# Decay and rate products, their sigmoids and cumulative sums inside the units of v, and two swapped buffers in the RWKV-7 scan

## What is computed

```python
rkv = einsum('btsd,sde->btse', xs[:, :, :3], w_rkv)          # r, k, v: three products of 1024 x 1024
logw = -softplus(-(w0 + tanh(xw @ w1) @ w2)) - 0.5           # decay
a = sigmoid(a0 + (xa @ a1) @ a2)                             # rate
kk = l2_normalize(heads(k * k_k))
k = k * (1.0 + (a - 1.0) * k_a)
y, s = rwkv7_recurrence(r, exp(-exp(logw)), k, v, -kk, kk * a, s0)   # heads of 64
# in the recurrence, for each token:
S = S * w_t + (S a_t) b_t + v_t k_t ;  y_t = S r_t
```

## Time and profile before

| | us |
|---|---|
| runs of the kernel before (3) | 2781.00, 2783.11, 2784.36 |
| median | 2783.11 |
| the profiled execution | 2780.13 |
| its span, first to last instruction | 2777.8 |
| PE busy in it | 2630.7 (95%) |

### The profile page before, as it was taken

The page is one execution under the profiler, slowest core; times in us unless marked ns, Lnnn a source line. Parts: engine busy times, 40 slices in busy tenths (PEclk is TensorE's granted clock), DMA queues, the critical chain, the costliest instruction groups (busy, mean ns, idle before and its releaser), DMA issues. The chain is left out here.

```text
span 2777.8 us, 62146 instructions
## 1 busy us (share of the span) xinstructions
PE 2630.7 (95%) x27185; PEld 2548.2 (92%) x27185; DVE 1146.0 (41%) x1458; ACT 892.2 (32%) x1281; POOL 1014.4 (37%) x478
## 2 busy tenths in 40 slices
PE   9999999997899999999999999999588889999998
PEld 8999998997888999999999999899378859999998
DVE  3333127845554533321533322631754455433313
ACT  4222224233323422222422222333533333422222
POOL 2444432332434244444244443133034352344442
PEclk9999999999998999999999999899689999999999
DMA  4222222221013222222222222122000022222321
GB/s 151 83 91 92 94 72 73 91 67 39 2 51 112 75 90 84 91 100 75 73 86 86 96 94 80 43 92 89 1 3 4 4 78 80 63 89 86 105 84 54
DMA packets 55195, 202.98 MB, mean 73 GB/s; under 512 B 6384, under 2 KB 8560, under 8 KB 55024
## 3 DMA queue, kind: packets, MB, share of 16 engines
q1 hardware_dynamic: 55024, 200.38, 22.0%
HBM read 190.68 MB, written 9.67 MB: 72 GB/s over the span
## 5 line engine op out<-in xcount | busy, mean ns | idle before, releaser
L317 POOL TENSOR_TENSOR wlo<-raw,whi 128x1024 fp32r<-128x1024 f32 (+1 forms) x261 | 709.0, 2716 | 1018.7 <-ACT whi L282 1018.7
L346 PE MATMUL ps<-xh,whi 128*128 128x272 f32 x3568 | 1031.2, 289 | 6.1 <-POOL wlo L317 4.2
L348 PE MATMUL ps<-xh,wlo 128*128 128x272 f32 x3568 | 1034.7, 290 | 0.0
L347 PE MATMUL ps<-xl,whi 128*128 128x272 f32 x3568 | 1027.3, 288 | 0.0
L346 PEld LDWEIGHTS ps<-xh,whi 128*128 128x128 f32 x3568 | 673.1, 189 | 9.5 <-issue 6.8
L347 PEld LDWEIGHTS ps<-xl,whi 128*128 128x128 f32 x3568 | 674.1, 189 | 0.0
L348 PEld LDWEIGHTS ps<-xh,wlo 128*128 128x128 f32 x3568 | 672.0, 188 | 0.0
L282 ACT ACTIVATE whi<-raw 128x1024 fp32r<-128x1024 f32 (+1 forms) x261 | 297.8, 1141 | 1103.4 <-PE ps L348 1099.6
L348 PE MATMUL ps<-mh,wlo 128*128 128x272 f32 x1408 | 406.1, 288 | 0.0
L346 PE MATMUL ps<-mh,whi 128*128 128x272 f32 x1408 | 405.8, 288 | 0.0
L347 PE MATMUL ps<-ml,whi 128*128 128x272 f32 x1408 | 405.4, 288 | 0.0
(11 more groups left out here) (494 smaller groups left out, 3393.9 us busy)
## 6 DMA issues: line engine op xcount, KB each, us to landing
raw<-w SPq DMA_DIRECT2D x245, 512.0 KB, 3.6
raw<-w SPq DMA_DIRECT2D x64, 704.0 KB, 4.0
mS<-state_gdn SPq DMA_DIRECT2D x8, 512.0 KB, 5.3
gdn_s_s<-mS SPq DMA_DIRECT2D x8, 512.0 KB, 2.7
h<-xT SPq DMA_DIRECT2D x4, 544.0 KB, 9.1
yT<-h SPq DMA_DIRECT2D x8, 272.0 KB, 2.2
go_r<-w SPq DMA_DIRECT2D x4, 512.0 KB, 5.5
S<-state_rwkv SPq DMA_DIRECT2D x8, 256.0 KB, 4.2
```

The lines of the kernel that those rows point to most:

```text
L317: pool.tensor_tensor(wlo[two][:, 0:kt * P], raw[slot][:, 0:kt * P], whi[two][:, 0:kt * P].bitcast(F32), ALU.subtract).then_inc(w_lo, 1)
L346: pe.matmul(o, wh, hi[:, r, :], start=(start and k == 0), stop=False)
L347: pe.matmul(o, wh, lo[:, r, :], start=False, stop=False)
L348: mm = pe.matmul(o, wl, hi[:, r, :], start=False, stop=(stop and k == kt - 1))
```

## The change

Names first. `inside` is a new argument of `unit_mm`: a function that is called ahead of each of the 16 steps of a unit (a step is three matmuls), and may put instructions of its own between them.

- **Key sums.** ACT squares tiles 0 to 3 after it has copied v's units 0 and 1, and tiles 4 to 7 after unit 2. PE sums them inside units 2 and 3, ahead of steps 6, 8, 10 and 12. The root follows on ACT after unit 3's copy.
- **Narrow products and sigmoids.** All 16 stand inside v's units: the first in unit 4 ahead of step 13, five each in units 5, 6 and 7 ahead of steps 2, 6, 9, 12 and 15. All use one PSUM pair (pair 3), so each waits for the sigmoid of the one before. ACT takes the sigmoids in batches between its copies and weight splits. They go to `cs` and `as_`, which lie where xn and dd, the shifted inputs, lay: mixing of v's input, their last reader, is over by then.
- **Cumulative sums.** DVE makes all eight in place in `cs`, ahead of the product with the spread roots, each as soon as its sigmoid is there. The reset mask moves to `tb[3]` and is loaded by SP between the weights of k and v, without the waits for the mixing of v's input.
- **The prep loop** keeps its products. Its temporaries are now `tb[0]`, `tb[1]` and `rs` for even tiles, two tiles in the gap below `after_x` and `lt1` for odd ones.
- **Scan.** Even levels go to ZL0 and odd ones to ZL1, so level 0 waits for `Zb` alone and level 1 for the transpose. The diagonal (L2625), which is in ZL1, now waits for the last doubling and not the one before it. The transpose of group 1's k goes to bank 1 and not 0, and each group of the first doubling waits for ACT's copies by itself. The two output additions of a chunk move from behind `state` to behind the first and the second doubling of the next chunk.

The diff, cut to its core:

```diff
-        def unit_mm(pe, name, u, j, out, hi, lo, k0=0, start=True, stop=True, between=None, between_half=1):
+        def unit_mm(pe, name, u, j, out, hi, lo, k0=0, start=True, stop=True, between=None, between_half=1,
+                    inside=None):
...
+                    if inside is not None:
+                        inside(kt * half + k)
...
-        tmp = [[place(f"pt{e}{i}", [P, 2, HALF], F32, at) for i in range(4)] for e in range(2)]
-        reset = place("reset", [P, T], F32, at)
+        tmp = [[tb[0], tb[1], rs], [above[0], above[1], lt1]]
+        cs, as_ = xn, dd
...
-                if i == 2:
-                    key_square_act(act, m)
+                if i == 2 and m in (1, 2):
+                    for j in range(4 * (m - 1), 4 * m):
+                        key_square_act(act, j)
+                if i == 2 and m == 3:
+                    root_ahead(act, 2)
+                    act.wait_ge(R["kq_mm"], past(R["kq_mm"], NM))
+                    act.activation(ROOTS, row_sums(6), ACT.Sqrt, bias=eps[:, 0:1]).then_inc(R["kq_rt"], 1)
+                    narrow_act(act, 0)
+                if i == 2 and 4 <= m < NM - 1:
+                    for n in range(5 * m - 19, 5 * m - 14):
+                        narrow_act(act, n)
...
+        def inside_v(pe, m):
+            def inside(step):
+                if m in (2, 3) and step in (6, 8, 10, 12):
+                    key_sum_pe(pe, 4 * (m - 2) + (step - 6) // 2)
+                if m == 4 and step == 13:
+                    narrow_pe(pe, 0)
+                if m > 4 and step in (2, 6, 9, 12, 15):
+                    narrow_pe(pe, 1 + 5 * (m - 5) + (2, 6, 9, 12, 15).index(step))
...
+        def narrow_pe(pe, n):
+            m, par = n // 2, n % 2
+            lo = 64 * par
...
+                pe.wait_ge(R["sg_cp"], past(R["sg_cp"], n))
+            for half in range(2):
+                mm = pe.matmul(pair(3)[:, half, :], wa2[lo:lo + 64, m * P:(m + 1) * P], lt1[lo:lo + 64, half, :], start=True, stop=True)
+            mm.then_inc(R["sg_mm"], 1)
+
+        def narrow_act(act, n):
+            dst, bias = (as_, V_A0) if n % 2 else (cs, V_W0)
+            act.wait_ge(R["sg_mm"], past(R["sg_mm"], n + 1))
+            act.activation(wh(dst, n // 2), pair(3), ACT.Sigmoid, bias=v(bias + n // 2)).then_inc(R["sg_cp"], 1)
...
+            for m in range(NM):
+                dve.wait_ge(R["sg_cp"], past(R["sg_cp"], 2 * m + 1))
+                c = whole(cs)[:, m, :]
+                dve.tensor_tensor_scan(c, flat(tb[3]), c, 0.0, ALU.mult, ALU.add).then_inc(R["scan"], 1)
...
-        VB, AB, BB, KB = (4, 2), (0, 3), (1, 4), (2, 0)
+        VB, AB, BB, KB = (4, 2), (0, 3), (1, 4), (2, 1)
...
-                    zl = ZL0 if i % 2 == 0 else ZL1
+                    zl = ZL1 if i % 2 == 0 else ZL0
...
+                    if c and i < 2:
+                        outputs(c - 1, i)
...
                         if l == 0:
                             pool.wait_ge(W["a_act"], past(W["a_act"], 5 * n + 1))
+                        elif l == 1:
                             pool.wait_ge(W["a_mm"], past(W["a_mm"], 8 * n + 8))
...
-                        zl = ZL1 if l % 2 == 0 else ZL0
+                        zl = ZL0 if l % 2 == 0 else ZL1
...
-                    pool.wait_ge(W["t_mm"], past(W["t_mm"], lev(c, 3, g)))
+                    pool.wait_ge(W["t_mm"], past(W["t_mm"], lev(c, 4, g)))
```

More of the change, by code:

```diff
@@ L1889, in trunk_kernel @@
         gap = at[0]
-        at = [after_x]
-        tmp = [[place(f"pt{e}{i}", [P, 2, HALF], F32, at) for i in range(4)] for e in range(2)]
-        reset = place("reset", [P, T], F32, at)
+        at = [gap]
+        above = [place(f"pt{i}", [P, 2, HALF], F32, at) for i in range(2)]
+        assert at[0] <= after_x
+        tmp = [[tb[0], tb[1], rs], [above[0], above[1], lt1]]
+        cs, as_ = xn, dd
         shout = place("shout", [P, NM, 1 + NB], F32, [after_x + 2 * NM * HALF * 4 * 2 + 512])
@@ L2076, in rkv_pe @@
                     continue
[L2077 to L2082, removed]
+                unit_mm(pe, name, m - m % 4, m % 4, rkv_pair(i, m), xh, xl, inside=inside_v(pe, m) if i == 2 else None)
+        def inside_v(pe, m):
[6 more added lines that the diff above has]
+                    narrow_pe(pe, 1 + 5 * (m - 5) + (2, 6, 9, 12, 15).index(step))
+            return inside
+        def narrow_pe(pe, n):
+            m, par = n // 2, n % 2
+            lo = 64 * par
+            if n == 0:
+                pe.wait_ge(R["w2_in"], past(R["w2_in"], 16))
+                pe.wait_ge(R["lora_cp"], past(R["lora_cp"], 2))
+                pe.wait_ge(R["kq_rt"], past(R["kq_rt"], 1))
+            else:
+                pe.wait_ge(R["sg_cp"], past(R["sg_cp"], n))
[6 more added lines that the diff above has]
+            act.activation(wh(dst, n // 2), pair(3), ACT.Sigmoid, bias=v(bias + n // 2)).then_inc(R["sg_cp"], 1)
         def lora_scale_dve(dve):
@@ L2210, in prep_pe @@
                 for half in range(2):
-                    mm = pe.matmul(pair(2 + m % 2)[:, half, :], M["headones"], tmp[m % 2][3][:, half, :], start=True, stop=True)
+                    mm = pe.matmul(pair(2 + m % 2)[:, half, :], M["headones"], tmp[m % 2][2][:, half, :], start=True, stop=True)
                 mm.then_inc(R["bo_mm"], 1)
@@ L2263, in prep_dve @@
             dve.wait_ge(R["kk_up"], past(R["kk_up"], NM))
-            dve.wait_ge(R["rm_in"], past(R["rm_in"], 16))
             for m in range(NM):
[L2266 to L2274, removed]
+                u0, u3, u6 = (t[:, :, :] for t in tmp[m % 2])
                 if m:
@@ L2547, in state, with outputs @@
                 dve.tensor_tensor(St[1 - cc][:, :, :], bank64(5), add, ALU.add).then_inc(W["s_up"], 1)
[L2548 to L2551 removed]
+            def outputs(c, g):
+                dve.wait_ge(W["y_mm"], past(W["y_mm"], 2 * c + g + 1))
+                dve.tensor_tensor(slot(RA, c, g), banks(6 + g, 1, P, P), slot(RA, c, g), ALU.add).then_inc(W["y_up"], 1)
             ident = cident[:, :].unsqueeze(1).broadcast_to([P, 8, 64])
@@ L2587, in scan_dve @@
                 state(NCH - 1, cc)
+            for g in range(2):
+                outputs(NCH - 1, g)
         def scan_pool(pool):
```

41 lines of the change are left out of this document (11 added, 30 removed).

## The result

The changed kernel takes a median of 2765.38 us (2763.69 to 2766.71, four runs) beside 2782.68 us of the kernel before (2781.0 to 2784.36, four runs): a ratio of 0.9934 with a 95% interval of 0.9918 to 0.9949. It is 17.3 us faster by the medians where 23.5 were forecast; the time lies inside the range of 2752 to 2769 us that was to hold 8 in 10, and 0.4 us outside the forecast's own band of 2753 to 2765, in the band that was given to three rivals. The profiled execution has a span of 2761.3 us, 16.5 less than before.

A forecast was written before the change was run, and what follows sets the result against it. PE was taken to bound v's units, a chain then DVE to bound prep, and a PE-ACT-DVE chain with POOL waits the scan. -26.3 + 13.8 - 11 = -23.5 us from 2783.11 gave 2759.6 us; 8-in-10 range 2752 to 2769.

The forecast's parts named there:

- Part 1: Prep, last matmul of v's units to first scan product: 51.6 us in place of 78.0, a saving of 26.3 us.
- the term of the sums: DVE's prep loop: taking the cumulative sums out saves 9.5 us.
- Part 2: v's units, where PE is the bound: added key sums, narrow products and a wait cost 13.8 us, bounds 10 to 19.
- Its claim on the narrow products' waits: v's units: a sigmoid's result takes 1.4 us, the next product stands 1.83 us later, so 0.4 us to spare.
- two take 0.57: v's units: a narrow product's two matmuls take 0.57 us, since three took 0.86 us at full clock.
- the 0.13 for the change of shape: v's units: 0.13 us per narrow product, as a key sum's change of shape cost beyond its row.
- The upper bound, 1.0: v's units: at most 1.0 us per narrow product, if the change of shape back and forth costs 0.43.
- Part 3: Scan: first doublings no longer wait for POOL's levels, 2.66 us earlier a chunk, 10.6 in four; 11 us taken, bounds 5 and 13.
- PE waiting for sigmoids: Rival, v's units: 15 waits of 0.5 us, 7.5 us, giving 2767; 0.20 together with the POOL-DVE and swap rivals.
- PE's clock halved: Rival, v's units 4 to 7: waits bring clock 0.50 to 0.54, 35 us more, 2795 us; chance 0.04.
- Exclusion between POOL and DVE in the scan: Rival, scan: two more collisions of 0.94 us a chunk, 7.5 us, 2767; 0.20 together with the sigmoid and swap rivals.
- That the swap does nothing: Rival, scan: another operand held the first doubling, 11 us less gained, 2771; 0.20 together with the sigmoid and POOL-DVE rivals.

The follow-up runs named there:

- the last experiment: The changed kernel with the eight cumulative sums back in DVE's prep loop: 2770.01 us, ratio 0.9964 to the kernel before.
- the pair: The changed kernel with decay and rate product of a tile side by side again, eight pairs inside v's units: 2756.09 us, ratio 0.9907 to the kernel before.
- the doubled product: The changed kernel with each narrow product made twice, in the same row group: 2780.26 us, ratio 0.9995 to the kernel before.
- the move alone: The kernel before with only the output additions moved behind the next chunk's first two doublings: 2781.09 us, ratio 1.0004.

## Why the prediction was right, and where it was not

**Part 1, right.** 51.6 us were forecast from the last unit product to the first scan product, 51.41 measured; the term of the sums, 9.5, is the 9.5 of the last experiment. That ACT and the bonus sums would not become late in the loop held too.

**Part 2, mis-sized by 9.5 us.** Its key sums held: seven of the eight in the changed kernel add 0.56 to 0.57 us, and key sum 4 adds 0.72, so that the wait forecast there as 0.3 was 0.15. Its claim on the narrow products' waits held too: PE's idle time in front of them names no sigmoid (us, times):

```profile
  issue: 0.8, 5
```

The term that failed is "two take 0.57": 0.86 us for x6 in the earlier trace rows were divided by three matmuls. In that stretch the decay product of a tile (rows 0 to 63) and its rate product (rows 64 to 127) stood next to each other and shared the time; the six records start in twos there, at 1956.98, 1957.21 and 1957.44. 0.57 is the price of a product that has a partner. The change takes the partner away, and a product by itself has four records of 0.23, in one row of 1.18 us. In the prediction's own sum, 1.18 with the 0.13 for the change of shape is the 1.31 that was measured, so the 0.13 held and 0.57 should have been 1.18. Eight records of the pair take 1.19 us and eight of the doubled product, in one row group, 2.10. The upper bound, 1.0, was formed from the change of shape alone and was too low for the same reason; the bounds for the part, 10 to 19, missed 23.3. The Trainium skill, page "TensorE: Matmul & The Clock Gate", section "Part 3: Packing small matmuls — row/col tiling", says that small matmuls whose inputs lie in different row groups run concurrently (the page measures tiles of 32 rows). The trace agrees for 64 rows, with 1.18 us for one product and 1.19 for two. The prediction did not use this rule, and it spoke against the change.

**Part 3, right, with chunk 0 mis-sized.** In chunk 3 group 0's first doubling moved up by 3.27 - 1.00 = 2.27 us against its transposes (2.3 forecast) and group 1's by 2.68 (2.66 forecast). The forecast counted 2.66 in four chunks; chunk 0 gave 1.35, since there the subtractions of both groups meet POOL's levels. Its sentence that only chunk 0 has POOL busy then was right, and it put no price on it. So 9.7 us and not 10.6 are the doublings' part of the 11.0 that came off the scan. The rest is not shown: the clock in the scan's middle rose from 0.97 to 1.00, but in the last 50 us of the same windows it went from 1.00 (2171.7 to 2221.7 before) to 0.97 (2165.4 to 2215.4 after). That the additions "cost nothing" at their new place fits the traces, in which PE's first doublings of chunks 1 to 3 do not wait for DVE. Without that cover they cost 1.3 us a chunk as forecast, but in three chunks, and 0.46 to 0.70 of each is the longer subtraction beside POOL, which the forecast did not have there: that the 1.3 fits is in part luck.

**The rivals.** PE waiting for sigmoids: no such wait. PE's clock halved: 1.00 throughout v's units. (Of the 0.50 to 0.54 given for it, show 0.54.) Exclusion between POOL and DVE in the scan: in the changed kernel in chunk 0 alone, at 1.00 and 0.91 us; it appears in the other chunks, at 1.11 to 1.35 us, when the additions are put back. That the swap does nothing: POOL's 11.8 us are gone, and the move alone gains nothing.

**The sum.** -26.6 + 23.3 - 11.0 = -14.3 us by the stages, -17.3 by the medians, -18.4 by the ratio with an interval from -22.8 to -14.2. What the 3 to 4 us between are can't be told from runs that begin the stage 4.7 us apart; it stays open. The stages alone would have put the median at 2783.11 - 14.3 = 2768.8 us, 9.2 over the forecast; that it lies only 5.8 over it is owed to these unexplained us, and that much of the hit is luck.

## What to carry to other kernels

A duration per instruction that is divided out of a row with a count holds only for the neighbours that stood there: before a matmul of 64 rows is moved, see whether the one beside it uses the other row group, and move the two together. An engine's work that leaves a loop where it is the bound for a place where it idles is worth its full time, as the cumulative sums show. And of operands made in a fixed order, those that depend on nothing late should come first; how much of that is kept depends on what the next engine still has to do ahead of them, as the output additions show.

## What the runs showed of the hardware

Two products of 64 rows in different row groups take 1.19 us together, in the same row group 2.10, and one alone 1.18; the records of the first start in twos, and both products end together. To break a run of 128-row products for a 64-row one and go back costs 0.39 us beside the product's own 0.92. The type of the operands changes there as well (the kernel declares the wide products' operands fp32r and the narrow ones' fp32), so the runs do not show that the shape alone costs it. The Trainium skill, page "TensorEngine Tiling (Array Packing)", section "Key Properties", says that a change of the tiling mode drains the engine; a cost at such a change agrees with that in kind, and the page gives no price.

One cumulative sum beside POOL's split of weights took 2.14 us and not 1.29: it started 1.42 us into a split that had 0.98 us to go. That looks like the exclusion of the earlier trace rows at another place, though no run tests it here. It delayed nobody: v's stage takes 61.42 us with the sums inside it and 61.46 without. DVE, then POOL, in the changed kernel:

```profile
1936.98 1.29 DVE L2284 TENSOR_TENSOR_SCAN xn<-tb,xn 128x544 f32<-128x544 f32 x1 [3.58 <-ACT xn L2120]
1941.85 2.14 DVE L2284 TENSOR_TENSOR_SCAN xn<-tb,xn 128x544 f32<-128x544 f32 x1 [3.58 <-ACT xn L2120]
```

```profile
1940.43 2.40 POOL L2003 TENSOR_TENSOR wlo<-raw,whi 128x1024 fp32r<-128x1024 f32 x1 [10.15 <-ACT whi L1996]
```
